# W2 of 15 of 16 feature chunks by Strassen's scheme, interleaved with the next chunk's W1

## The reference

```python
xn = rms_norm(h, norm_mlp[l])
u = jax.nn.relu(xn @ mlp_w1[l])        # 512 x 2048 times 2048 x 8192
h = h + (u * u) @ mlp_w2[l]            # 512 x 8192 times 8192 x 2048
...
return rms_norm(h, norm_final)
```

## Time and profile before

| | before |
|---|---|
| median of 3 runs | 2750.11 us (2747.82 to 2755.4) |
| profiled execution: its own time | 2753.86 us |
| profiled execution: span, first to last instruction | 2751.8 us |
| mean granted TensorE clock | 0.989 of 2.4 GHz |
| busy share of the span: PE, DVE, ACT, POOL | 97%, 45%, 30%, 5% |
| MLP stretch on PE, first matmul to the last units | 1321.14 to about 2740 us |

### The profile page before, as it was taken

The page is one execution under the profiler, slowest core; times in us unless marked ns, Lnnn a source line. Parts: engine busy times, 40 slices in busy tenths (PEclk is TensorE's granted clock), DMA queues, the critical chain, the costliest instruction groups (busy, mean ns, idle before and its releaser), DMA issues.

```text
span 2751.8 us, 44317 instructions
## 1 busy us (share of the span) xinstructions
PE 2680.3 (97%) x18352; PEld 2141.6 (78%) x18352; DVE 1229.6 (45%) x1908; ACT 811.8 (30%) x1340; POOL 133.8 (5%) x238
## 2 busy tenths in 40 slices
PE   9999999999999899998999999999999999999997
PEld 7877777777777666886888887878878878788886
DVE  6266666666436555335433332433323333324334
ACT  5222222222126434335421221312213222122233
POOL 4000111001131100000000000000000000000000
PEclk9999999999999899999999999999999999999999
DMA  5311111111245422221223222222222322222332
GB/s 167 121 54 49 48 54 48 44 53 47 64 130 193 161 85 63 93 92 64 85 99 100 92 100 93 94 98 95 97 93 92 100 93 93 91 100 92 100 100 100
DMA packets 72447, 250.06 MB, mean 91 GB/s; under 512 B 8960, under 2 KB 9088, under 8 KB 71104
## 3 DMA queue, kind: packets, MB, share of 16 engines
q1 hardware_dynamic: 65232, 222.62, 24.7%
q0 software_dynamic: 7024, 24.56, 2.7%
HBM read 236.93 MB, written 10.22 MB: 90 GB/s over the span
## 4 chain that ended last, share of the span: by engine, by line
PE 95%; DVE 2%; ACT 1%; issue 1%; DMA 1%; DVEq 0%; ACTq 0%; POOL 0%; SPq 0%; POOLq 0%
PE ps L1200 28%; PE ps L1201 26%; PE ps L1202 26%; PE ps L1218 9%; PE ps L1404 1%; PE ps L1427 1%; PE ps L1414 1%; PE ps L1212 1%; DMA h<-in_a_line 0%; PE ps L1266 0%; PE ps L1263 0%; PE ps L1255 0%; DVE w_lo L746 0%; PE ps L1272 0%; PE ps L1245 0%
## 5 line engine op out<-in xcount | busy, mean ns | idle before, releaser
L746 DVE TENSOR_TENSOR w_lo<-w_raw,w_hi 128x1024 fp32r<-128x1024 f32 (+2 forms) x440 | 505.2, 1149 | 1097.8 <-ACT w_hi L452 1097.7
L452 ACT ACTIVATE w_hi<-w_raw 128x1024 fp32r<-128x1024 f32 (+2 forms) x440 | 438.9, 998 | 1568.5 <-PE ps L1202 1560.7
L1200 PE MATMUL ps<-act_hi,w_hi 128*128 128x512 f32 x1792 | 729.8, 407 | 1.8 <-DVE w_lo L746 1.7
L1201 PE MATMUL ps<-act_lo,w_hi 128*128 128x512 f32 x1792 | 702.5, 392 | 12.7 <-issue 12.7
L1202 PE MATMUL ps<-act_hi,w_lo 128*128 128x512 f32 x1792 | 702.3, 392 | 0.0
L1200 PE MATMUL ps<-w_hi,mid_hi 128*128 128x512 f32 x1088 | 425.2, 391 | 3.9 <-DVE w_lo L746 2.5
L1202 PE MATMUL ps<-w_hi,mid_lo 128*128 128x512 f32 x1088 | 423.8, 390 | 0.0
L1201 PE MATMUL ps<-w_lo,mid_hi 128*128 128x512 f32 x1088 | 423.8, 390 | 0.0
L1200 PEld LDWEIGHTS ps<-act_hi,w_hi 128*128 128x128 f32 x1792 | 337.5, 188 | 94.7 <-issue 10.6
L1201 PEld LDWEIGHTS ps<-act_lo,w_hi 128*128 128x128 f32 x1792 | 338.1, 189 | 81.8 <-issue 18.7
L1202 PEld LDWEIGHTS ps<-act_hi,w_lo 128*128 128x128 f32 x1792 | 338.1, 189 | 72.5
(11 more groups left out here) (290 smaller groups left out, 2336.8 us busy)
## 6 DMA issues: line engine op xcount, KB each, us to landing
w_raw<-in_w_rest SPq DMA_DIRECT2D x320, 512.0 KB, 3.3
w_raw<-in_w_pairs SPq DMA_DIRECT2D x112, 384.0 KB, 3.0
x_t<-in_x_turned SPq DMA_DIRECT2D x8, 512.0 KB, 9.9
qk<-scr_qkv POOLq DMA_DIRECT2D x16, 256.0 KB, 3.0
h<-in_x POOLq DMA_DIRECT2D x4, 1024.0 KB, 7.1
out<-h SPq DMA_DIRECT2D x4, 1024.0 KB, 3.9
scr_qkv<-pad POOLq DMA_DIRECT2D x15, 256.0 KB, 4.0
w_raw<-in_w_lora SPq DMA_DIRECT2D x8, 288.0 KB, 7.9
```

The costliest lines, as they stand in the source:

```text
L452: return nc.scalar.activation(dst, src, ACT.Copy, scale=scale)
L746: V.tensor_tensor(dst, w_raw[:, slot, 0:dst.shape[-1]], high.bitcast(F32), ALU.subtract).then_inc(s["w_split"], 1)
L1200: mm(dst, a_hi, b_hi, start=start, stop=False)
L1201: mm(dst, a_hi, b_lo, start=False, stop=False)
```

## The change

The MLP is cut in 16 chunks of 512 features. For chunks 0 to 14, W2 is done by Strassen's scheme in Winograd's form: the 512 squared features by 512 tokens are a 2x2 arrangement of quarters (A11, A12, A21, A22: 256 tokens by 256 features), W2's rows of the chunk too (B11, B12, B21, B22: 256 features by 512 columns, once for each half of the columns of a quarter). Seven products take the place of eight, with sums S1, S2, S4 on the token side and T-sums (BT, and B11, B12, B21 overwritten in place) on the weight side. So a chunk has 14 products, numbered 0 to 13 below, each of 12 matmuls of the same shape as before (`down_op`). GpSimd makes the sums (`token_sums`, `weight_sums`); ACT makes the high parts of sums and weights (`sum_his`, `op_hi`), DVE the low parts (`sum_low`, `op_lo`) and the additions to `h`, two banks a product (`op_add`). Accumulating banks are shared between products (`SET_OF`). The factor 1/rms is now applied before the square (`rectified`, with `inv_row`); its row comes from one more matmul in chunk 0.

On PE the body of a chunk is: W1 units 0 and 1 of chunk c, products 0 and 1 of chunk c-1, unit 2, products 2 and 3, unit 3, and so on to unit 7, then products 12 and 13. The loop over chunks holds three bodies (`FOLD`) and runs five times. The last chunk's W2 is done with eight units as before. W1 unit u of a chunk is called unit u below.

```diff
-MLP_CHUNKS = 8
-G_ALL = G_MLP + 4 * MLP_CHUNKS
+MLP_CHUNKS = 16
+G_LAST = G_MLP + MLP_CHUNKS
+G_ALL = G_LAST + 1
 FT = D_FF // MLP_CHUNKS // P
+FOLD = 3
...
+        s5 = alloc(m_tmp)
+        sum_hi = s5("sum_hi", [P, 7, 2, SEQ // 2], F32R)
+        raw_tmp = ExitStack()
+        sums = alloc(raw_tmp)("sums", [P, 7, 2, SEQ // 2])
+        raw_tmp.close()
+        sum_lo = s5("sum_lo", [P, 7, 2, SEQ // 2], F32R)
+        b_raw = s5("b_raw", [P, 5, 2 * REST_W])
+        b_hi, b_lo = s5("b_hi", [P, 2, 2 * REST_W], F32R), s5("b_lo", [P, 2, 2 * REST_W], F32R)
+        gain_out = s5("gain_out", [P, D])
+        one_t = s5("one_t", [P, P])
+        m_tmp.close()
...
+        B11, B12, B21, B22, BT = range(5)
+        A11, A12, A21, A22, S1, S2, S4 = range(7)
+        M1, M2, M6, M5 = (A11, B11, True, 0, 0), (A12, B21, True, 0, 0), (S2, BT, False, 0, 1), (S1, B11, True, 1, 1)
+        M7, M3, M4 = (A21, B12, False, 1, 1), (S4, B22, False, 0, 1), (A22, B21, False, 1, 0)
+        PRODUCTS = ((M1, M2, M6, M5, M7, M3, M4), (M1, M2, M6, M5, M7, M4, M3))
+        SET_OF = (0, 1, 0, 1, 0, 1, 0, 1, 0, 1, 0, 1, 1, 0)
+        READY_AS = {A11: 1, A12: 2, S2: 3, S1: 4, A21: 5, S4: 6, A22: 7}
+        def product(n):
+            return PRODUCTS[n // 7][n % 7]
+        def op_used_at(c, n):
+            return 14 * c + n + 3
+        def op_evac_at(c, n):
+            return 28 * c + 2 * n + 4
...
+            def down_next(c, n):
+                b = {3: B11, 4: B12, 5: B22, 6: B21, 10: B11, 11: B12, 12: B21, 13: B22}[n]
+                sp.wait_ge(s["op_split"], 14 * c + n + 1)
+                if n < 7:
+                    down_block(c, 1, b)
+                else:
+                    down_block(c + 1, 0, b)
...
+            def token_sums(c):
+                def combine(i, dst, a, b, op):
+                    nc.gpsimd.tensor_tensor(quarter(sums, dst), quarter(sums, a), quarter(sums, b), op).then_inc(s["s_ready"], 1)
+                pool.wait_ge(s["raw_done"], 4 * c + 4)
+                combine(0, S1, A21, A22, ALU.add)
+                pool.wait_ge(s["s_ready"], 4 * c + 1)
+                combine(1, S2, S1, A11, ALU.subtract)
+                combine(2, A21, A11, A21, ALU.subtract)
+                pool.wait_ge(s["s_ready"], 4 * c + 2)
+                pool.wait_ge(s["op_used"], 14 * c + 2)
+                combine(3, S4, A12, S2, ALU.subtract)
+            def weight_sums(c, half):
+                k = 2 * c + half
+                def combine(dst, a, b):
+                    nc.gpsimd.tensor_tensor(b_raw[:, dst, :], b_raw[:, a, :], b_raw[:, b, :],
+                                            ALU.subtract).then_inc(s["t_ready"], 1)
+                pool.wait_ge(b_landed[B12], 16 * (k + 1))
+                pool.wait_ge(s["op_split"], 7 * k + 1)
+                combine(B11, B12, B11)
+                pool.wait_ge(b_landed[B22], 16 * (k + 1))
+                pool.wait_ge(s["t_ready"], 4 * k + 1)
+                combine(BT, B22, B11)
+                combine(B12, B22, B12)
+                pool.wait_ge(s["t_ready"], 4 * k + 2)
+                pool.wait_ge(s["op_split"], 7 * k + 2)
+                combine(B21, B21, BT)
+            with pool.Fori(0, (MLP_CHUNKS - 1) // FOLD) as j:
+                for i in range(FOLD):
+                    token_sums(FOLD * j + i)
+                    for half in range(2):
+                        weight_sums(FOLD * j + i, half)
...
+            def up_hi(c, u):
+                g = G_MLP + c
+                hi(u % RAW, 2 * g + u // RAW + 1, rest_slot(w_hi, u), UNITS * g + u - SPL + 1)
+            def op_hi(c, n):
+                k, (_, b, _, _, _) = 2 * c + n // 7, product(n)
+                p = n % 7
+                if p in (0, 1) or b == B22:
+                    act.wait_ge(b_landed[b], 16 * (k + 1))
+                else:
+                    act.wait_ge(s["t_ready"], 4 * k + {B11: 1, BT: 2, B12: 3, B21: 4}[b])
+                act.wait_ge(s["op_used"], op_used_at(c, n - 2))
+                copy(b_hi[:, n % 2, :], b_raw[:, b, :]).then_inc(s["op_hi"], 1)
+            def mid_squares(c):
+                def square_hi(a):
+                    nc.scalar.activation(quarter(sum_hi, a), quarter(sums, a), ACT.Square).then_inc(s["mh_done"], 1)
+                def square(a):
+                    nc.scalar.activation(quarter(sums, a), quarter(sums, a), ACT.Square).then_inc(s["raw_done"], 1)
+                act.wait_ge(s["r_done"], 4 * c + 2)
+                square_hi(A11)
+                square(A11)
+                square(A21)
+                act.wait_ge(s["r_done"], 4 * c + 4)
+                square_hi(A12)
+                square(A12)
+                square_hi(A22)
+                square(A22)
+            def sum_his(c):
+                for i, a in ((2, S2), (1, S1), (3, A21), (4, S4)):
+                    act.wait_ge(s["s_ready"], 4 * c + i)
+                    copy(quarter(sum_hi, a), quarter(sums, a)).then_inc(s["mh_done"], 1)
+            def mlp_body(c):
+                op_hi(c - 1, 0)
+                op_hi(c - 1, 1)
+                sum_his(c - 1)
+                up_hi(c, 2)
+                up_hi(c, 3)
+                for pair in range(6):
+                    op_hi(c - 1, 2 * pair + 2)
+                    op_hi(c - 1, 2 * pair + 3)
+                    up_hi(c + (pair + 4) // UNITS, (pair + 4) % UNITS)
+                mid_squares(c)
...
+            def up_lo(c, u):
+                lo(UNITS * (G_MLP + c) + u, u % RAW, rest_slot(w_lo, u), rest_slot(w_hi, u))
+            def op_lo(c, n):
+                dve.wait_ge(s["op_hi"], 14 * c + n + 1)
+                V.tensor_tensor(b_lo[:, n % 2, :], b_raw[:, product(n)[1], :], b_hi[:, n % 2, :].bitcast(F32),
+                                ALU.subtract).then_inc(s["op_split"], 1)
+            def op_add(c, n):
+                _, _, _, i, j = product(n)
+                cols = slice(j * 1024 + n // 7 * 512, j * 1024 + n // 7 * 512 + 512)
+                dve.wait_ge(s["op_used"], op_used_at(c, n))
+                dve.wait_ge(s["op_evac"], op_evac_at(c, n - 1))
+                for t in range(2):
+                    dst = h[:, 2 * i + t, cols]
+                    V.tensor_tensor(dst, dst, bank(2 * SET_OF[n] + t), ALU.add).then_inc(s["op_evac"], 1)
+            def rectified(c, m):
+                if m < 3:
+                    dve.wait_ge(s["f_done"], 3 * c + m + 1)
+                else:
+                    dve.wait_ge(s["w_used"], UNITS * (G_MLP + c + 1))
+                j, k = m // 2, m % 2
+                V.scalar_tensor_tensor(sums[:, j:j + 3:2, k, :], bank(4 + m).rearrange("p (i n) -> p i n", i=2), 0.0,
+                                       inv_row.rearrange("p (i n) -> p i n", i=2), ALU.max, ALU.mult).then_inc(s["r_done"], 1)
+            def sum_low(c, a, high, sums_read):
+                dve.wait_ge(s["mh_done"], 7 * c + high)
+                if sums_read:
+                    dve.wait_ge(s["s_ready"], 4 * c + sums_read)
+                V.tensor_tensor(quarter(sum_lo, a), quarter(sums, a), quarter(sum_hi, a).bitcast(F32),
+                                ALU.subtract).then_inc(s["ml_done"], 1)
+            def mlp_body(c):
+                op_lo(c - 1, 0)
+                op_lo(c - 1, 1)
+                for a, high, sums_read in ((A11, 1, 3), (A12, 2, 4), (S2, 4, 4), (S1, 5, 4), (A21, 6, 4), (S4, 7, 4), (A22, 3, 4)):
+                    sum_low(c - 1, a, high, sums_read)
+                up_lo(c, 2)
+                up_lo(c, 3)
+                for pair in range(6):
+                    for n in (2 * pair, 2 * pair + 1):
+                        op_add(c - 1, n)
+                        op_lo(c - 1, n + 2)
+                    if pair == 5:
+                        rectified(c, 0)
+                        rectified(c, 1)
+                    up_lo(c + (pair + 4) // UNITS, (pair + 4) % UNITS)
+                dve.wait_ge(s["op_used"], op_used_at(c - 1, 12))
+                rectified(c, 2)
+                rectified(c, 3)
+                op_add(c - 1, 12)
+                op_add(c - 1, 13)
...
+            for a, high, squared_as in ((A11, 1, 1), (A21, 4, 2), (A12, 2, 3), (A22, 3, 4)):
+                dve.wait_ge(s["raw_done"], 4 * (MLP_CHUNKS - 1) + squared_as)
+                sum_low(MLP_CHUNKS - 1, a, high, 0)
...
+                combos = [(k, m) for k in range(2) for m in range(FT)]
+                if u == UNITS - 1 or u == 0 and not opening:
+                    combos = [(k, m) for m in range(FT) for k in range(2)]
...
+                    elif kt == 0:
+                        pe.wait_ge(s["r_done"], 4 * c + m - 3)
+                    last = split_mm(bank(4 + m), wh[:, k, mp], wl[:, k, mp], act_hi[:, kt, :], act_lo[:, kt, :],
+                                    kt == 0, kt == KT - 1)
+                    if kt == KT - 1 and m < 3:
+                        last.then_inc(s["f_done"], 1)
...
+            def down_op(c, n):
+                a, _, start, _, _ = product(n)
```

(24 more changed lines are left out.)

328 lines of the change are left out of this document (188 added, 140 removed).

## The result

| | before | after |
|---|---|---|
| median | 2752.97 us (5 runs, 2747.82 to 2755.58) | 2776.48 us (5 runs, 2768.1 to 2778.67) |
| ratio, 95% interval | | 1.0083 (1.0062 to 1.0103) |
| profiled execution, span | 2751.8 us | 2773.0 us |
| mean granted TensorE clock | 0.989 | 0.982 |

The changed kernel is slower by 23.5 us, where +36 was forecast. The page of the kernel after, part 1: PE has 358 matmuls fewer in the records (360 were taken out, one was added) and 54 us less busy time than the earlier trace rows, and the span is 21 us longer. DVE and GpSimd have become busier, but neither is near the bound.

A forecast was written before the change was run, and what follows sets the result against it. PE, busy 97% of the span, was taken as the bound. Terms: -81.6 - 4.1 + 117 - 7 + 6.5 + 4.1 + 0.5 = +35.4 us, giving 2786 us on the median, range 2714 to 2812.

The forecast's parts named there:

- 360 matmuls fewer, 81.6 us: PE, W2 of 15 chunks: 168 matmuls instead of 192 each, at 0.2267 us, taking 81.6 us off.
- Product 13, 2.8 us idle in each of 15 chunks: PE before product 13 waits for DVE's additions of product 12, with nothing to cover it: 2.8 us a chunk.
- By turns, unit 2's low part at 28.1 on the clock of unit 7's end: DVE low parts and GpSimd sums alternate, so unit 2's low part ends 28.1 us after unit 7 ends on PE.
- Turning point: two weight sums among the low parts and unit 2 is in time: At most two weight sums among DVE's low parts leave unit 2 ready; three make it about 1 us late.
- the rule of the Trainium skill as the prediction read it: DVE/GpSimd SBUF contention: first issued holds the ports; back-to-back low parts could keep GpSimd out, making unit 2's term 0.
- Idle time at unit 2, 3.5 us, and 1.5 us of slow pace beside it: PE waits 3.5 us a chunk for unit 2's low part; slow pace counts once a chunk, 1.5 us.
- the 7.8 of the sum: Forecast cost per chunk on PE: 2.8 and 3.5 us idle plus 1.5 slow pace, 117 us over 15 chunks.
- the granted clock was to be under 0.97 in the MLP: Sign expected in the profile after: PE's granted clock under 0.97 in the MLP.
- Four loop starts at 4.1 each, 7 us of it hidden at unit 2, so 9.4 net: PE loop starts: 2.5 us idle plus 1.6 slow each; in four following chunks the pause hides 1.8 us, -7 together.
- First chunk, 10 us idle: First chunk, unit 2: PE arrives 8.3 us earlier without products 12 and 13, so 10 us idle, not 3.5: +6.5.
- Last chunk, one more idle time: Last chunk's first W2 unit waits for two low parts behind product 13's additions: +4.1 us.
- +35.4: Whole forecast change in us, the sum of all terms, giving 2789 on the profiled execution and 2786 on the median.

The follow-up runs named there:

- e10_order_gate: Changed kernel, product 13 waiting for product 11's additions, unit 2's low part earlier on DVE, two weight sums held until product 2's low part: 2673.0 us, ratio 0.9713.
- e1: Changed kernel with product 13 waiting for product 11's additions instead of product 12's: 2782.5 us, ratio 1.0127.
- e2: Changed kernel with GpSimd's four half-0 weight sums held until DVE has written the low part of unit 2: 2716.2 us, ratio 0.9886.
- e4: Changed kernel with each weight sum cut to 8 columns and memsets for the rest, so products take wrong weights: 2714.8 us, ratio 0.9871.
- e5: Changed kernel with two half-0 weight sums left early and the other two held until unit 2's low part: 2725.0 us, ratio 0.9901.

## Why the prediction was right, and where its sizes were off

- *360 matmuls fewer, 81.6 us*: right. The chunks have 360 matmuls each, and e10_order_gate has 82.5 us for them.
- *Product 13, 2.8 us idle in each of 15 chunks*: 2.66 us, 15 times. But as long as unit 2 is late it costs nothing by itself: e1 takes it away and the idle time at unit 2 takes its place. The prediction added the two as if each had its own price; its sum was right only because both were there.
- *By turns, unit 2's low part at 28.1 on the clock of unit 7's end*: that clock's zero is 1540.99 here (product 13 starts at 1546.37, less 2.66 idle and 2.72 of product 12), so the low part comes at 1568.95 - 1540.99 = 28.0. The steps between are there as well: the token sums start at 6.4, when ACT's squares were forecast to end at 6.6; the four weight sums take 11.73 / 4 = 2.9 us each (forecast 2.7 from one to the next). e2, e4 and the table of turns show it as the cause, with 2.2 us lost by DVE for each weight sum, the value that was taken between two DVE operations.
- *Turning point: two weight sums among the low parts and unit 2 is in time*: e5 shows just that.
- *By the rule of the Trainium skill as the prediction read it, the term would be 0 if low parts issued back to back kept GpSimd out*: they didn't keep it out. In the kernel after DVE's seven low parts stand ready in a row, and the four weight sums take turns with the first of them. The other half of that section of the Trainium skill (SBUF — State Buffer, "Who interferes with whom"), that the contention is with a GpSimd instruction which reads SBUF, agrees with e4, where memsets hold nothing up.
- *Idle time at unit 2, 3.5 us, and 1.5 us of slow pace beside it*: this is the term that was off most. With 360 x 0.2267 = 81.6 us of matmuls, the three chunks in which PE keeps its pace after product 13 (3.19 us idle at unit 2, slow pace behind it) are 89.4 to 89.7 us long, some 7.9 over their matmuls and just the 7.8 of the sum. In seven others PE is slow after product 13 instead; that slow pace is hidden in the wait at unit 2, which shrinks to 1.7 us, none to speak of comes behind it, and the chunk is 88.15 to 88.2 us long, 6.5 over. On average the ten chunks without a loop start are 6.95 over, 0.85 less than forecast: some 13 us in the sum. With it went a sign: the granted clock was to be under 0.97 in the MLP, and it was 0.98 from 1320 to 2740 us.
- *Four loop starts at 4.1 each, 7 us of it hidden at unit 2, so 9.4 net*: right in size by luck, not by its mechanism. The four chunks behind a loop start are 89.84, 91.54, 91.21 and 89.92 us long, 2.1 more than the ten others on average, 8.3 us in all. But PE's own pause, 2.5 us at each in the forecast, is 0.96 and 0.86 us at two of them and nothing at the others. What the prediction did not have is DVE's pause of 1.8 to 2.0 us: unit 2 starts 0.2 to 1.8 us later behind product 13 than in the other chunks, some 4 us in all, and the rest is slow pace behind unit 2.
- *First chunk, 10 us idle*: 7.67 at unit 2 and 1.66 at product 0. *Last chunk, one more idle time*: 2.72 us at its first unit.

So the two waits in each chunk and their causes were the forecast ones, and of the 14 us between +35.4 and the spans' +21.2 some 13 are the slow pace in the chunks and 1 the loop starts.

## What to carry to other kernels

Where two engines take turns at a shared resource, count how many of the other's long instructions can slip in ahead of the one that is waited for, and hold them back by a wait behind it; here that, one wait relaxed and one instruction moved turned +0.8% into -2.9% without taking work off any engine. An idle time that is followed by another wait on a chain of its own is not a cost by itself: ask what that chain starts from before a wait is removed. Don't carry the price of a loop's jump from one body to another: see whether instructions are loaded at it, and look for the pause on every engine, not on PE alone.
